# Reading order of the token operand in the 512-column matrix products of a two-block float32 model

## The chip, the cores and the metric

The kernel is one program on one core of a Trainium2 chip. The metric is the device time of one execution in microseconds (us); lower is better. TensorE (PE) multiplies matrices, VectorE (DVE) and ScalarE (ACT) do elementwise work, GpSimd (POOL) a few masks and powers, and SyncE (SP) starts the transfers from memory. SBUF is the on-chip memory that the engines read, PSUM the one that TensorE writes.

## What is computed

A token matrix of 256 tokens by 1024 features goes through a first block (gated pooling and forgetting attention) and a second block of two layers, with four feed-forward parts among other things. Nearly all of the work of the products that are changed lies in those four:

```python
D_MODEL, SEQ, D_FF = 1024, 256, 2816

def swiglu(x, w_gu, w_down):
    gate, up = jnp.split(x @ w_gu, 2, axis=-1)
    return (jax.nn.silu(gate) * up) @ w_down
...
x = x + 0.5 * swiglu(rms_norm(x, ffn1_norm[l]), ffn1_w_gu[l], ffn1_w_down[l])
```

All data are float32. The kernel multiplies in a faster TensorE format (`F32R`, "fp32r" in the rows) of lower precision, and gets precision back by splitting each operand in a high part (the value rounded to that format) and a low part (what is left): a product is then w_hi·x_hi + w_lo·x_hi + w_hi·x_lo.

## The kernel before

A weight matrix arrives in units of up to 11 blocks of 128 x 128. SP brings two units at a time into `raw`; ACT rounds a unit into `w_hi` (L594), DVE subtracts and leaves the rest in `w_lo` (L1157), four units deep each. TensorE then runs through the blocks `k` of a unit and adds their products up in one of four PSUM banks of 512 columns, `main0` to `main3`. A unit's end lets ACT and DVE take the result and prepare a later unit.

There are two ways to make the three products of a block:

- **Triples** (`triple`, L2138 to L2140): three products of 256 columns (the tokens), into the same 256 columns of a bank. They are used outside the feed-forward parts, and in a few units in them.
- **Pairs**: one product of `w_hi` with high and low tokens together, 512 columns, that puts w_hi·x_hi in columns 0 to 255 of the bank and w_hi·x_lo in 256 to 511; then one product of `w_lo` with the high tokens, 256 columns, added to columns 0 to 255. The two halves of the bank are added when ACT and DVE take them out. `project_halves` (L2165 and L2167) does this for gate and up, 8 blocks to a unit; `down` in `ffn` (L2523 and L2525) for the second matrix, 11 blocks to a unit.

The tokens lie in SBUF in two ways. For gate and up it is `xs`, of shape 128 x 8 x 2 x 256: for one block `k`, the 256 high tokens (1024 bytes of each partition) and right behind them the 256 low ones, so that the 512 columns are one run of addresses. For down it is `h_both`, of shape 128 x 2 x 22 x 256: the low tokens of a block lie 22528 bytes behind its high ones, so that the 512 columns are two runs. In both, the destination is one run of 512 columns. `enter` (the first two units of two of the feed-forward parts) makes pairs as well, with code of its own that the change doesn't touch.

The order of the instructions is written out by hand for each engine; semaphores tie the engines together. TensorE waits for `lo_ready` at the start of a unit and for `evac` where it takes a bank again.

Of the kernel before, what the change touches and what calls it, by code (L numbers as in the profile page):

```python
# [16 lines left out]
KC = D // P  # L17
# [5 lines left out]
FT = FF // P  # L23
# [134 lines left out]
def program(nc, dram, out):  # L158
    with ExitStack() as ctx:
# [7 lines left out]
        xs, _ = place("xs", at + 32, [P, KC, 2, SEQ], F32R)  # L167
# [6 lines left out]
        w_hi, at = place("w_hi", at, [P, RING, UNIT], F32R)  # L174
# [18 lines left out]
        h_both, at = place("h_both", free0, [P, 2, FT, SEQ], F32R)  # L193
# [227 lines left out]
        def piece(tensor, u, b, n=1):  # L421

            return tensor[:, u % RING, b * P:(b + n) * P]
# [1705 lines left out]
        def _(pe):  # L2129
# [6 lines left out]
            def triple(dst, a_hi, a_lo, b_hi, b_lo, first, last):  # L2136
# [2 lines left out]
                pe.matmul(dst, a_lo, b_hi, start=False, stop=False)  # L2139
                return pe.matmul(dst, a_hi, b_lo, start=False, stop=last)  # L2140

            def unit_begin(u, off=0):
                pe.wait_ge(lo_ready, u + 1 + off)

# [14 lines left out]
            def project_halves(u, bank, off=0, first=None):  # L2159

                unit_begin(u, off)
                for k in range(KC):
                    if first is not None:
                        pe.wait_ge(xg_ready, first + k + 1)
                    pe.matmul(bank[:, :], piece(w_hi, u, k), xs[:, k], start=k == 0, stop=k == KC - 1,  # L2165
                              skip_group_check=True)
                    ins = pe.matmul(bank[:, 0:SEQ], piece(w_lo, u, k), xs_hi[:, k], start=False, stop=k == KC - 1,  # L2167
                                    skip_group_check=True)
                unit_end(ins)
# [176 lines left out]
            bank = side[2]  # L2346
# [10 lines left out]
            for u in range(40):  # L2357
# [16 lines left out]
                if 8 <= u < 12:  # L2374
# [9 lines left out]
                    for kk in range(2):  # L2384
                        k = 2 * j + kk
# [104 lines left out]
            def ffn(which):  # L2490
                f, u0, t0 = FFNS.index(which), first_unit("w_gu_" + which), FIRST_TILE["gu_" + which]

                def turn(i, first=None):
                    if first is not None and which != "a1":
                        enter(u0, [bank_of(t0 + j) for j in range(2)], (xs_hi, xs_lo) if which == "b2" else (xs,), first,
                              2 if which == "b2" else 1, None if which == "b2" else FFN_NORM[which])
                    for j in range(2 if first is not None and which != "a1" else 0, 4):
                        if which == "b2" and first is not None:
                            project(u0 + j, bank_of(t0 + j)[:, 0:SEQ], xs_hi, xs_lo,
                                    within=(KC - 2, lambda: norm_sum(FFN_NORM[which])) if j == 2 else None)  # L2500
                        else:
                            project_halves(u0 + j, bank_of(t0 + j, i * 4), i * 4, first if j == 0 else None)
                        if first is not None and which == "a1" and j == 0:
                            norm_sum(FFN_NORM[which])

                if which != "b1":
                    turn(0, XG0["ffn_" + which])
                with pe.Fori(0 if which == "b1" else 1, (FT - FFN_FIRST[which]) // 2) as i:
                    turn(i)
                u0, t0 = first_unit("w_down_" + which), FIRST_TILE["down_" + which]  # L2510

                def down(m, i=0, joined_parts=True):
                    bank = bank_of(t0 + m, i * 4)
                    for j in range(2):
                        u = u0 + 2 * m + j
                        pe.wait_ge(h_ready, f * FT + FT // 2 + j * (FT // 2 - 2))
                        unit_begin(u, i * 8)
                        for b in range(FT // 2):
                            k = j * (FT // 2) + b
                            if k >= FT - 2:  # L2520
                                pe.wait_ge(h_ready, f * FT + k + 1)
                            if joined_parts:
                                pe.matmul(bank[:, :], piece(w_hi, u, b), h_both[:, :, k, :], start=k == 0,  # L2523
                                          stop=k == FT - 1, skip_group_check=True)
                                ins = pe.matmul(bank[:, 0:SEQ], piece(w_lo, u, b), h_hi[:, k, :], start=False,  # L2525
                                                stop=k == FT - 1, skip_group_check=True)
                            else:
                                ins = triple(bank[:, 0:SEQ], piece(w_hi, u, b), piece(w_lo, u, b),
                                             h_hi[:, k, :], h_lo[:, k, :], k == 0, k == FT - 1)
                        unit_end(ins)  # L2530

                if which == "b2":
                    for m in range(KC):
                        down(m, joined_parts=m < KC - 1)
                else:
                    with pe.Fori(0, 2) as i:
                        for m in range(4):
                            down(m, i)
# [583 lines left out]
```

## Time and profile before

| | |
|---|---|
| time, median of 3 runs | 1196.64 us (1196.5 to 1197.19) |
| span of the profiled execution, first to last instruction | 1195.0 us |
| the median less that span (start and end around it; the profiled execution's own total is not listed) | 1.6 us |
| TensorE busy with matmuls | 1187.3 us (99%), 7956 of them |
| DVE busy | 934.7 us (78%) |
| ACT busy | 730.4 us (61%) |
| mean granted TensorE clock | 0.999 of full speed |

A matmul's row gives its start and a modelled duration, from the first column that goes in to the last that comes out; the next one starts before it ends. How fast TensorE gets on is therefore read from one start to the next, not from the durations. Where a group's busy time is given for products that overlap the next of the same group, it is the time that the whole sequence took.

### The profile page before, as it was taken

How to read it: one execution, taken by the hardware profiler on the slowest of the kernel's cores; microseconds unless marked ns; L12 is line 12 of the kernel's file. 1: busy time of each engine (PE TensorE's matmuls, PEld its weight loads, DVE VectorE, ACT ScalarE, POOL GpSimd, SP SyncE). 2: the span in 40 equal slices, each digit the busy share in tenths (PEclk: the TensorE clock that was granted, in tenths of full speed). 3: DMA queues.
4: the chain of work that ended last, by engine and by line, in shares of the span. 5: the costliest groups of instructions: out<-in, count | busy, mean ns of one | idle time of the engine just before them, and what ended most of it. 6: DMA issues, size and time to landing. Idle time of an engine off the chain costs nothing.

```text
span 1195.0 us, 22393 instructions
## 1 busy us (share of the span) xinstructions
PE 1187.3 (99%) x7956; PEld 1089.4 (91%) x7956; DVE 934.7 (78%) x1617; ACT 730.4 (61%) x1211; POOL 77.9 (7%) x91
## 2 busy tenths in 40 slices
PE   9999999999999999999999999999999999999998
PEld 9899999888888999999888889988888989888887
DVE  7766788988876788688988767888876787888853
ACT  7564746666654588567666645666664567666642
POOL 4460000000000000610000000000000000000000
PEclk9999999999999999999999999999999999999999
DMA  8545655554654445115555743655663423555730
GB/s 329 184 142 187 232 189 177 186 208 176 230 214 154 141 170 188 41 36 177 211 178 204 258 151 123 211 176 194 219 239 135 150 91 125 195 205 178 255 131 36
DMA packets 48143, 209.92 MB, mean 176 GB/s; under 512 B 3486, under 2 KB 4908, under 8 KB 43596
## 3 DMA queue, kind: packets, MB, share of 16 engines
q1 hardware_dynamic: 46720, 204.96, 48.7%
q10 hardware_dynamic: 1356, 4.07, 1.0%
q8 instruction: 41, 0.67, 0.2%
q14 instruction: 26, 0.21, 0.0%
HBM read 207.90 MB, written 1.13 MB: 175 GB/s over the span
## 4 chain that ended last, share of the span: by engine, by line
PE 93%; DVE 4%; ACT 1%; issue 1%; DMA 1%; DVEq 0%; SPq 0%; ACTq 0%
PE main L2165 25%; PE main L2167 13%; PE main L2523 13%; PE main L2138 8%; PE main L2139 8%; PE main L2140 8%; PE main L2525 7%; DVE w_lo L1157 1%; PE side L2303 1%; PE main L2566 1%; PE side L2566 1%; PE side L2277 1%; PE main L2682 1%; PE main L2854 1%; PE main L2858 1%
## 5 line engine op out<-in xcount | busy, mean ns | idle before, releaser
L1157 DVE TENSOR_TENSOR w_lo<-raw,w_hi 128x1024 fp32r<-128x1024 f32 (+3 forms) x365 | 466.8, 1287 | 5.0 <-ACT w_hi L594 3.8
L2165 PE MATMUL main<-xs,w_hi 128*128 128x512 f32 x1328 | 461.3, 390 | 0.2 <-DVE xs L1191 0.2
L594 ACT ACTIVATE w_hi<-raw 128x1024 fp32r<-128x1024 f32 (+2 forms) x363 | 402.5, 1111 | 68.3 <-PE main L2140 53.0
L2167 PE MATMUL main<-xs,w_lo 128*128 128x256 f32 x1328 | 374.5, 282 | 0.0
L2165 PEld LDWEIGHTS main<-xs,w_hi 128*128 128x128 f32 x1328 | 249.2, 188 | 53.2 <-DVE w_lo L1157 0.7
L2167 PEld LDWEIGHTS main<-xs,w_lo 128*128 128x128 f32 x1328 | 251.0, 189 | 0.0
L2523 PE MATMUL main<-h_both,w_hi 128*128 128x512 f32 x682 | 236.6, 390 | 0.0
L2525 PE MATMUL main<-h_both,w_lo 128*128 128x256 f32 x682 | 192.3, 282 | 0.0
L2523 PEld LDWEIGHTS main<-h_both,w_hi 128*128 128x128 f32 x682 | 128.0, 188 | 26.8
L2525 PEld LDWEIGHTS main<-h_both,w_lo 128*128 128x128 f32 x682 | 128.9, 189 | 0.0
L2138 PE MATMUL main<-xs,w_hi 128*128 128x256 f32 x368 | 105.4, 286 | 0.0
L2139 PE MATMUL main<-xs,w_lo 128*128 128x256 f32 x368 | 102.9, 280 | 0.0
L2140 PE MATMUL main<-xs,w_hi 128*128 128x256 f32 x368 | 102.7, 279 | 0.0
L2138 PE MATMUL main<-xg,w_hi 128*128 128x256 f32 (+1 forms) x288 | 82.7, 287 | 0.3 <-DVE w_lo L1157 0.3
L2139 PE MATMUL main<-xg,w_lo 128*128 128x256 f32 (+1 forms) x288 | 81.0, 281 | 0.0
L2140 PE MATMUL main<-xg,w_hi 128*128 128x256 f32 (+1 forms) x288 | 81.0, 281 | 0.0
L1511 DVE TENSOR_TENSOR hid<-main,hid 128x256 f32<-128x256 f32 x84 | 35.6, 424 | 50.9 <-ACT hid L800 50.9
L800 ACT ACTIVATE hid<-main 128x256 f32<-128x256 f32 x84 | 32.3, 384 | 69.9 <-PE main L2167 69.9
L612 ACT ACTIVATE xs<-x,par 128x256 fp32r<-128x256 f32 (+1 forms) x48 | 23.9, 508 | 78.5 <-DVE x L1484 66.9
L2138 PEld LDWEIGHTS main<-xs,w_hi 128*128 128x128 f32 x368 | 69.2, 188 | 0.4 <-issue 0.2
L2139 PEld LDWEIGHTS main<-xs,w_lo 128*128 128x128 f32 x368 | 69.2, 188 | 0.1
L2140 PEld LDWEIGHTS main<-xs,w_hi 128*128 128x128 f32 x368 | 69.2, 188 | 0.0
(505 smaller groups left out, 1869.6 us busy)
## 6 DMA issues: line engine op xcount, KB each, us to landing
raw<-in_w_gu_a SPq DMA_DIRECT2D x44, 1024.0 KB, 5.2
raw<-in_w_gu_b SPq DMA_DIRECT2D x44, 1024.0 KB, 5.2
raw<-in_w_down_a SPq DMA_DIRECT2D x16, 1408.0 KB, 6.1
raw<-in_w_down_b SPq DMA_DIRECT2D x16, 1408.0 KB, 6.0
raw<-in_w_in SPq DMA_DIRECT2D x15, 1024.0 KB, 5.4
raw<-in_w_in_a SPq DMA_DIRECT2D x13, 1024.0 KB, 5.2
raw<-in_w_gates SPq DMA_DIRECT2D x4, 1024.0 KB, 5.1
raw<-in_w_up SPq DMA_DIRECT2D x4, 1024.0 KB, 5.2
```

Of the source, the lines that this page charges most:

```text
L594: act.activation(w_hi[:, u % RING, 0:n], raw[:, s % RAW, u % 2, 0:n], ACT.Copy).then_inc(hi_ready, 1)
L800: act.activation(dst, main[(t0 + n) % 4][:, SEQ:2 * SEQ], ACT.Copy).then_inc(low_half, 1)
L1157: return dve.tensor_tensor(dst, src, hi.bitcast(F32), ALU.subtract)
L1511: dve.tensor_tensor(dst, main[(t0 + n) % 4][:, 0:SEQ], dst, ALU.add).then_inc(evac, 1)
L2138: pe.matmul(dst, a_hi, b_hi, start=first, stop=False)
L2139: pe.matmul(dst, a_lo, b_hi, start=False, stop=False)
L2140: return pe.matmul(dst, a_hi, b_lo, start=False, stop=last)
L2165: pe.matmul(bank[:, :], piece(w_hi, u, k), xs[:, k], start=k == 0, stop=k == KC - 1, skip_group_check=True)
L2167: ins = pe.matmul(bank[:, 0:SEQ], piece(w_lo, u, k), xs_hi[:, k], start=False, stop=k == KC - 1, skip_group_check=True)
L2523: pe.matmul(bank[:, :], piece(w_hi, u, b), h_both[:, :, k, :], start=k == 0, stop=k == FT - 1, skip_group_check=True)
L2525: ins = pe.matmul(bank[:, 0:SEQ], piece(w_lo, u, b), h_hi[:, k, :], start=False, stop=k == FT - 1, skip_group_check=True)
L2566: ins = pe.matmul(dst[:, i * P:(i + 1) * P], lhs(i), rhs(i), start=first, stop=True, skip_group_check=not first)
```

## The change

Two helpers turn the operands' views. `parts_in_turn(v, n)` reads `n` high tokens, then the `n` low ones that belong to them, then the next `n` high ones, and so on; `in_turn(bank, n)` writes in the same order, so that each result lands in the column where it landed before. Gate and up use runs of 32 columns (16 runs to a product), down runs of 128 (4 runs). Number, kind and order of the instructions of all engines stay as they are, and so do the places of all data.

```diff
+            def in_turn(bank, n):
+                return bank[:, :].rearrange("p (i b n) -> p b i n", i=2, n=n)
+
+            def parts_in_turn(v, n):
+                return v.rearrange("p i (b n) -> p b i n", n=n)
...
-                    pe.matmul(bank[:, :], piece(w_hi, u, k), xs[:, k], start=k == 0, stop=k == KC - 1,
+                    pe.matmul(in_turn(bank, 32), piece(w_hi, u, k), parts_in_turn(xs[:, k], 32), start=k == 0, stop=k == KC - 1,
                               skip_group_check=True)
                     ins = pe.matmul(bank[:, 0:SEQ], piece(w_lo, u, k), xs_hi[:, k], start=False, stop=k == KC - 1,
                                     skip_group_check=True)
...
                             if joined_parts:
-                                pe.matmul(bank[:, :], piece(w_hi, u, b), h_both[:, :, k, :], start=k == 0,
-                                          stop=k == FT - 1, skip_group_check=True)
+                                pe.matmul(in_turn(bank, 128), piece(w_hi, u, b), parts_in_turn(h_both[:, :, k, :], 128),
+                                          start=k == 0, stop=k == FT - 1, skip_group_check=True)
```

## Rows read from the trace of the kernel before

**Rows 1.** Page, part 1: busy us (share of the span) xinstructions
```profile
PE 1187.3 (99%) x7956; PEld 1089.4 (91%) x7956; DVE 934.7 (78%) x1617; ACT 730.4 (61%) x1211; POOL 77.9 (7%) x91
```

**Rows 2.** Page, part 4: the chain that ended last
```profile
PE 93%; DVE 4%; ACT 1%; issue 1%; DMA 1%; DVEq 0%; SPq 0%; ACTq 0%
```

**Rows 3.** Page, part 5: the four products of pairs; busy, mean ns | idle before
```profile
L2165 PE MATMUL main<-xs,w_hi 128*128 128x512 f32 x1328 | 461.3, 390 | 0.2 <-DVE xs L1191 0.2
L2167 PE MATMUL main<-xs,w_lo 128*128 128x256 f32 x1328 | 374.5, 282 | 0.0
...
L2523 PE MATMUL main<-h_both,w_hi 128*128 128x512 f32 x682 | 236.6, 390 | 0.0
L2525 PE MATMUL main<-h_both,w_lo 128*128 128x256 f32 x682 | 192.3, 282 | 0.0
```

**Rows 4.** Busy time by stretch, gate and up: PE, PEld, DVE, ACT, POOL, PEclk, DMA, GB/s
```profile
230.00:330.00 100.00, 100.00 (x579) 88.67 (x578) 85.16 (x148) 64.03 (x110) 0.00 (x0) 1.00 0.59 209
```

**Rows 5.** Products on xs (L2165) that started in 230 to 330: ns min/median/max, first, last
```profile
L2165 PE MATMUL main<-xs,w_hi x290: 390/390/390, 229.8 to 329.9; 128*128 128x512 f32 x145
```

**Rows 6.** Timeline of PE, first and last of those 290: start us, us
```profile
229.75 0.39 PE L2165 MATMUL main<-xs,w_hi 128*128 128x512 f32 x1
...
329.94 0.39 PE L2165 MATMUL main<-xs,w_hi 128*128 128x512 f32 x1
```

**Rows 7.** Products on h_both (L2523) in 342 to 398, and their first and last
```profile
L2523 PE MATMUL main<-h_both,w_hi x160: 390/390/390, 341.7 to 396.8; 128*128 128x512 f32 x160
...
341.73 0.39 PE L2523 MATMUL main<-h_both,w_hi 128*128 128x512 f32 x1
...
396.85 0.39 PE L2523 MATMUL main<-h_both,w_hi 128*128 128x512 f32 x1
```

**Rows 8.** Timeline of PE, two pairs of gate and up
```profile
299.78 0.39 PE L2165 MATMUL main<-xs,w_hi 128*128 128x512 f32 x1
300.01 0.28 PE L2167 MATMUL main<-xs,w_lo 128*128 128x256 f32 x1
300.13 0.39 PE L2165 MATMUL main<-xs,w_hi 128*128 128x512 f32 x1
300.36 0.28 PE L2167 MATMUL main<-xs,w_lo 128*128 128x256 f32 x1
```

**Rows 9.** Timeline of PEld (weight loads) in the same stretch
```profile
300.13 0.19 PEld L2167 LDWEIGHTS main<-xs,w_lo 128*128 128x128 f32 x1
300.36 0.19 PEld L2165 LDWEIGHTS main<-xs,w_hi 128*128 128x128 f32 x1
```

**Rows 10.** Timeline of PE, triples on xg: first products of triple 1 and 30
```profile
99.91 0.28 PE L2138 MATMUL main<-xg,w_hi 128*128 128x256 f32 x1
...
110.06 0.28 PE L2138 MATMUL main<-xg,w_hi 128*128 128x256 f32 x1
```

**Rows 11.** The same on cat_hi_a, cat_lo_a: triple 1 and triple 56
```profile
530.15 0.29 PE L2138 MATMUL main<-cat_hi_a,w_hi 128*128 128x256 f32 x1
...
549.59 0.28 PE L2138 MATMUL main<-cat_hi_a,w_hi 128*128 128x256 f32 x1
```

**Rows 12.** The same with weights as columns, tokens held: triple 1 and triple 14
```profile
208.04 0.28 PE L2138 MATMUL main<-w_hi,mem_hi 128*128 128x256 f32 x1
...
212.66 0.28 PE L2138 MATMUL main<-w_hi,mem_hi 128*128 128x256 f32 x1
```

## The prediction

> **What bounds the kernel now.** I read the busy shares first: TensorE has a matmul under way for 1187.3 of 1195.0 us, DVE for 78%, ACT for 61% [rows 1]. That alone doesn't say that TensorE is the limit, so the chain that ended last comes next: 93% of it is TensorE, 4% DVE [rows 2]. In a stretch of gate and up, 230 to 330 us, TensorE is never idle, DVE is busy 85.16 of 100 us, ACT 64.03, and the granted clock is 1.00 of full speed, that is the 2.4 GHz level [rows 4]. The four lines of the pairs had 0.2 us of idle time before them in all [rows 3]. So the time is the sum of the steps from one product's start to the next, and what the change does to the time is what it does to that step.
>
> The steps are read from starts. The 290 products on `xs` between 229.75 and 329.94 us make 289 pairs in 100.19 us, 346.68 ns each [rows 5, 6]. The 160 products on `h_both` from 341.73 to 396.85 us make 159 pairs in 55.12 us, 346.67 ns each [rows 7]. The whole kernel agrees: the busy time of the 512-column products, which overlap from pair to pair, is 461.3 us for 1328 (347.4 ns each, waits included) and 236.6 us for 682 (346.9 ns) [rows 3]. Within a pair some 230 ns pass from the 512-column start to the 256-column one and some 120 ns from there to the next pair [rows 8]. The 768 columns of a pair need 768 / 2.4 = 320.0 ns at the granted clock. So 26.7 ns of each pair is over-time; over 1328 + 682 = 2010 pairs that is 53.7 us. The change can't take away more than this by reading the same columns in another order.
>
> **The change part by part.** It adds and removes no instruction, transfer or wait, and no data move to another place. It changes two things in 2010 products.
>
> *Reading.* Each product's columns are read in more runs. Call the passage from one run to the next a break. For `xs` there were none and there are 15; for `h_both` there was one (from the high tokens to the low ones, 22528 bytes on) and there are three. That is 15 x 1328 + 2 x 682 = 21,284 more breaks. What does a break cost? The trace has the comparison: a pair on `xs` without a break takes 346.68 ns, a pair on `h_both` with one takes 346.67 ns [rows 5 to 7]. The rounding of the starts to 0.01 us leaves 0.03 ns open in the first and 0.06 ns in the second, so a break costs at most 0.08 ns, and at most 0.08 x 21,284 = 1.7 us in all. I take zero, because the two sorts of pairs agree.
>
> *Writing.* The destination was one run of 512 columns everywhere and becomes 16 runs (gate and up) or 4 (down): 15 x 1328 + 3 x 682 = 21,966 breaks. No product of before writes with a break inside it, so this is bounded by neighbours. From below: nothing, as on the reading side; a gain is treated with the first rival. From above: a break can't well cost more than a whole new product with new weights does. A triple of 256-column products on `xg` takes (110.06 - 99.91) / 29 = 350.0 ns [rows 10], 116.7 ns a product of which 106.7 are columns: 10.0 ns of over-time per product start. At 10.0 ns a break it would be +220 us. Between 0 and 10 ns I take zero: it is the value of the nearest row, a break within one product, while the upper end is that of another event. A price in between, one column time a break, is the second rival.
>
> On the writing side stands also a rule of the Trainium skill, in "Advanced Engine Details and Errata", section "Memory Cachelines": PSUM is reached in lines of two float32 values, and "any non-contiguous AP significantly slows down matmuls". No row before has such a destination. The same section asks for every two consecutive elements to be contiguous, and runs of 32 and 128 columns meet that, so by this reading the sum stays at zero; by the first sentence taken literally it is the last rival below.
>
> *Other engines.* ACT and DVE read the bank after the pair's last product, and the results lie where they lay. If TensorE gets slower they wait more; if it gets faster by 2%, DVE's 85% in gate and up becomes 87%, so nothing else would take over at once [rows 4].
>
> Sum: 1195.0 + 0 (0 to 1.7 for reading) = 1195.0 us of span, and with the 1.6 us by which the runs' median stands above the span, 1196.6 us.
>
> **The rivals.**
>
> *Faster: part of the over-time goes away.* The 26.7 ns are not a fixed price. Products of the same shape at the same clock take 350.0 ns a triple on `xg` [rows 10], (549.59 - 530.15) / 55 = 353.5 ns on `cat_hi_a` and `cat_lo_a` [rows 11], and (212.66 - 208.04) / 13 = 355.4 ns where weights are the columns and tokens are held [rows 12]. Only what is read from where differs. A weight load runs beside each product from its start on [rows 8, 9], so both readings share something that depends on addresses, and an order that takes high and low tokens in turn goes through the addresses in another rhythm. The smallest step between these rows is about 3.4 ns for 768 columns. One such step down in each pair gives 2010 x 3.4 = 6.8 us, 1189.8 us; two give 1183.0 us; one in gate and up alone 4.5 us. Against it: the pairs take 346.7 ns on both token arrays, though one lies in one run and the other in two, and the step is the same in each of hundreds of pairs. The chance is 0.30, of which 0.06 for more than two steps.
>
> *Slower: a break costs one column time.* If the next run's first column goes in one clock late, because reading or writing has to set up a new start, a break costs 1 / 2.4 = 0.42 ns. On the writing side's count that is 21,966 x 0.42 = 9.2 us, 1205.8 us: 8.3 us of it in gate and up, where a product would take 6.3 ns more. It decides against no change from 2.4 / 21,966 = 0.11 ns a break. For it speaks that the trace shows no destination with breaks, and that 16 runs in 213 ns ask for a new start every 13 ns; against it that the one break in the reading of `h_both` costs nothing that can be seen. The chance is 0.19.
>
> *Slower: the other rhythm costs a step.* The first rival with the other sign: 3.4 ns more a pair, 1203.4 us. The rows give the sign no preference, except that the place with the largest over-time per column in them is the triple of rows 12, not the pair, so there is room upwards. The chance is 0.07.
>
> *Slower by far: a destination in runs is written at a much lower rate.* At the upper end of the writing side, 10.0 ns a break, it would be 1196.6 + 220 = 1416 us. The row of `h_both` can't exclude it, since its break is in the reading only. The chance is 0.02. This is the result that the skill's sentence quoted above would give if it held for runs of any length.
>
> *The change does nothing*, because the lists of addresses are worked off column by column and a run's end is no event at all. That is the forecast's own mechanism and gives its time.
>
> **How the numbers follow.** No change 0.42 (1196.6 us; by its own bounds 1194.3 to 1199.0), faster 0.30, slower by a column time 0.19, slower by a step 0.07, far slower 0.02. About 0.2%, 2.4 us, is what a measurement of this kernel can tell from no change. Faster by more than that is 0.30, within it 0.42, slower 0.28. The likeliest case gives 1196.6 us. The range reaches down to the two steps of the first rival, 1183, and up to the column time a break, 1206; beyond it lie 0.06 below and, with half of the spread around the column time, some 0.10 above.
>
> **What would show it.** In the profile of the changed kernel the starts of the 512-column products decide. If I am right, 290 products on `xs` still take 100.19 us and the busy time of that group stays at 461.3 us, that of `h_both` at 236.6 us. If a break costs a column time, a pair of gate and up takes 352.9 ns and one of down 347.9: gate and up suffer, down hardly. If over-time is given back, the pairs come below 346.7 ns, and the triples, which are not touched, stay at 350.0 and 353.5 ns. A difference between gate and up and down tells how the length of a run matters. The step from a 512-column start to the 256-column one must change and the other way round not, if the cost sits in the product with runs. What would make the forecast wrong is above all that a rhythm can't be read from rows of another rhythm, and that nothing before shows a destination in runs.

## The result: 8.6 us slower

| | before | after |
|---|---|---|
| time, median of 4 runs | 1196.59 us (1196.50 to 1197.19) | 1205.20 us (1205.07 to 1205.43) |
| ratio | 1 | 1.0071, interval 1.0059 to 1.0084 |
| span of the profiled execution | 1195.0 us | 1203.4 us |
| products of gate and up, 1328 of 512 columns: busy with their sequence | 461.3 us | 470.0 us |
| products of down, 682 of 512 columns: the same | 236.6 us | 236.6 us |

The change costs 0.7%, clear of what a measurement can tell from nothing, where no change was forecast. The forecast was wrong.

### The profile page after: what moved, and what is told of

It is laid out like the page before. It is cut to its first block, busy times and chain, and to the rows that moved or that the text cites. A ratio compares the mean times of both kernels' runs of the same rounds, so it can differ in the third digit from the quotient of the medians.

```text
span 1203.4 us, 22393 instructions
## 1 busy us (share of the span) xinstructions
PE 1196.4 (99%) x7956; PEld 1088.1 (90%) x7956; DVE 935.7 (78%) x1617; ACT 729.4 (61%) x1211; POOL 77.9 (6%) x91
## 4 chain that ended last, share of the span: by engine, by line
PE 95%; DVE 3%; ACT 1%; issue 1%; DVEq 0%; ACTq 0%
PE main L2171 26%; PE main L2173 13%; PE main L2529 13%; PE main L2138 8%; PE main L2140 8%; PE main L2139 8%; PE main L2531 7%; PE side L2309 1%; DVE w_lo L1157 1%; PE main L2572 1%; PE side L2572 1%; PE side L2283 1%; PE main L2688 1%; PE main L2860 1%; PE main L2864 1%; PE main L2862 1%
## 5 line engine op out<-in xcount | busy, mean ns | idle before, releaser
L2171 PE MATMUL main<-xs,w_hi 128*128 128x512 f32 x1328 | 470.0, 398 | 0.1
L2173 PE MATMUL main<-xs,w_lo 128*128 128x256 f32 x1328 | 371.9, 280 | 0.0
L2171 PEld LDWEIGHTS main<-xs,w_hi 128*128 128x128 f32 x1328 | 249.3, 188 | 63.3 <-DVE xs L1191 0.5
L2173 PEld LDWEIGHTS main<-xs,w_lo 128*128 128x128 f32 x1328 | 249.3, 188 | 0.0
L2529 PE MATMUL main<-h_both,w_hi 128*128 128x512 f32 x682 | 236.6, 390 | 0.0
L2531 PE MATMUL main<-h_both,w_lo 128*128 128x256 f32 x682 | 192.3, 282 | 0.0
L2529 PEld LDWEIGHTS main<-h_both,w_hi 128*128 128x128 f32 x682 | 128.0, 188 | 26.9
L2531 PEld LDWEIGHTS main<-h_both,w_lo 128*128 128x128 f32 x682 | 128.9, 189 | 0.0
```

The costliest lines, as they stand in the source:

```text
L2171: pe.matmul(in_turn(bank, 32), piece(w_hi, u, k), parts_in_turn(xs[:, k], 32), start=k == 0, stop=k == KC - 1, skip_group_check=True)
L2529: pe.matmul(in_turn(bank, 128), piece(w_hi, u, b), parts_in_turn(h_both[:, :, k, :], 128), start=k == 0, stop=k == FT - 1, skip_group_chec ...
```

## The profile after

The page's busy shares, the chain that ended last, and the groups of the pairs (L2171 and L2173 are the former L2165 and L2167, L2529 and L2531 the former L2523 and L2525; the columns are those of [rows 1 to 3]):

```profile
PE 1196.4 (99%) x7956; PEld 1088.1 (90%) x7956; DVE 935.7 (78%) x1617; ACT 729.4 (61%) x1211; POOL 77.9 (6%) x91
...
PE 95%; DVE 3%; ACT 1%; issue 1%; DVEq 0%; ACTq 0%
...
L2171 PE MATMUL main<-xs,w_hi 128*128 128x512 f32 x1328 | 470.0, 398 | 0.1
...
L2173 PE MATMUL main<-xs,w_lo 128*128 128x256 f32 x1328 | 371.9, 280 | 0.0
...
L2529 PE MATMUL main<-h_both,w_hi 128*128 128x512 f32 x682 | 236.6, 390 | 0.0
L2531 PE MATMUL main<-h_both,w_lo 128*128 128x256 f32 x682 | 192.3, 282 | 0.0
```

TensorE still sets the end, and all of the loss is in gate and up: 470.0 - 461.3 = 8.7 us against the first of [rows 3]. Down is where it was, to 0.1 us. The span grew by 8.4 us, a little less: TensorE was idle for 7.0 us (1203.4 - 1196.4) where it had been for 7.7.

The steps are read from starts, as in [rows 5, 6]. The timeline of PE in gate and up, with the number of 512-column products that started in 230 to 330 us (the two ends stand on the same product line, 283 pairs apart):

```profile
L2171 PE MATMUL main<-xs,w_hi x284: 397/397/398, 229.8 to 329.8; 128*128 128x512 f32 x142
...
229.76 0.40 PE L2171 MATMUL main<-xs,w_hi 128*128 128x512 f32 x1
230.00 0.28 PE L2173 MATMUL main<-xs,w_lo 128*128 128x256 f32 x1
230.12 0.40 PE L2171 MATMUL main<-xs,w_hi 128*128 128x512 f32 x1
...
329.76 0.40 PE L2171 MATMUL main<-xs,w_hi 128*128 128x512 f32 x1
```

100.00 us for 283 pairs are 353.4 ns a pair, where it was 346.7. The whole of it lies between the start of the 512-column product and that of the next one, some 236 ns where some 228 were; the other step got a nanosecond shorter. ACT and DVE only wait longer for it: ACT's wait for `hid` in all, 69.9 us before, is

```profile
ACT hid L800 <- PE main L2173: 76.8, 76, 1.1
```

**How the experiments are read.** The four feed-forward parts a1, a2, b1 and b2 run one after the other, and several kernels below do another thing in each. One view gives a row for each part: the busy time of the 512-column products alone, with their number. Since they overlap from pair to pair, this is the time of the whole sequence of pairs. The difference to the same row of the kernel before, divided by the number, is what a pair costs more. The columns of a row are: window, its length, PE busy with the number of products, PEld busy with the number of loads, clock, DMA share, GB/s. Gate and up, before and then after:

```profile
212.00:340.00 128.00, 122.62 (x352) 66.04 (x352) 1.00 0.57 202
555.00:680.00 125.00, 116.68 (x336) 63.08 (x336) 1.00 0.57 201
760.00:880.00 120.00, 110.98 (x320) 60.08 (x320) 1.00 0.59 206
1010.00:1130.00 120.00, 111.00 (x320) 60.04 (x320) 1.00 0.58 200
```

```profile
212.00:340.00 128.00, 124.88 (x352) 66.09 (x352) 1.00 0.56 198
555.00:684.00 129.00, 118.92 (x336) 63.08 (x336) 1.00 0.56 198
760.00:888.00 128.00, 113.11 (x320) 60.07 (x320) 1.00 0.57 201
1015.00:1140.00 125.00, 113.12 (x320) 60.08 (x320) 1.00 0.56 198
```

So the change costs 6.4, 6.7, 6.7 and 6.6 ns a pair in a1 to b2. (In a1 the first products wait for weights anyway, which hides a part.) The numbers of the other kernels are given as such differences. Down has rows of the same kind; before, in a1 and b2, and after, in a1:

```profile
334.00:400.00 66.00, 61.06 (x176) 33.02 (x176) 1.00 0.49 175
1124.00:1184.00 60.00, 53.43 (x154) 28.89 (x154) 1.00 0.30 111
```

```profile
336.00:402.00 66.00, 61.07 (x176) 33.04 (x176) 1.00 0.49 173
```

Each kernel up to the last two (down128 and turns64) ran once. Where a kernel below changes gate and up with a view or for reading or writing alone, down is as in the kernel before.

## Experiments

Two theories stood at the start. The second rival of the prediction: each break between runs costs a column time. It gives nearly the right total, 1205.8 us, but 1.25 ns a pair for down, which took none. And the third: another rhythm of addresses costs a step. Beside them stood the question which side it is, reading or writing.

### Reading or writing

```diff
-                    pe.matmul(in_turn(bank, 32), piece(w_hi, u, k), parts_in_turn(xs[:, k], 32), ...
+                    pe.matmul(bank[:, :], piece(w_hi, u, k), parts_in_turn(xs[:, k], 32), ...      # read32
...
+                    pe.matmul(in_turn(bank, 32), piece(w_hi, u, k), xs[:, k], ...                  # write32
```

> Gate and up read in turns of 32 columns but write one run of 512; down as in the kernel before. The low and high sums so land in other columns than the later steps take them from, so the values are not the reference's; the work is the same. Theory R (the cost sits in reading): a pair of gate and up takes 353.4 ns as in the changed kernel, time about 1205. Theory W (it sits in writing PSUM in runs): 346.7 ns as before, time about 1196.6. If each side has a part, in between.

> The other half alone: gate and up read one run of 512 columns and write in turns of 32 (values not the reference's, for the same reason). Theory R: 346.7 ns a pair, about 1196.6. Theory W: 353.4 ns a pair, about 1205.

Read32 took 1205.57 us, write32 1196.69 us, beside 1197.28 us for the kernel before on the same chip. The rows of b1 and b2 of read32:

```profile
760.00:888.00 128.00, 113.11 (x320) 60.06 (x320) 1.00 0.57 201
1015.00:1140.00 125.00, 113.13 (x320) 60.07 (x320) 1.00 0.57 197
```

and of write32:

```profile
760.00:880.00 120.00, 110.98 (x320) 60.04 (x320) 1.00 0.59 206
1010.00:1130.00 120.00, 111.00 (x320) 60.08 (x320) 1.00 0.57 201
```

The cost is in the reading, all of it. A destination in 16 runs of 32 columns costs nothing that can be seen. So one of the two things that by the prediction's last sentence could make it wrong, a destination in runs, was free. The other one was the rhythm of the reading.

### The length of a run

```diff
+GU_RUN = {'a1': 8, 'a2': 16, 'b1': 64, 'b2': 128}
+DOWN_RUN = {'a1': 8, 'a2': 16, 'b1': 32, 'b2': 64}
...
-                    pe.matmul(in_turn(bank, 32), piece(w_hi, u, k), parts_in_turn(xs[:, k], 32), ...
+                    pe.matmul(in_turn(bank, n), piece(w_hi, u, k), parts_in_turn(xs[:, k], n), ...
...
-                                pe.matmul(in_turn(bank, 128), piece(w_hi, u, b), parts_in_turn(h_both[:, :, k, :], 128),
+                                pe.matmul(in_turn(bank, DOWN_RUN[which]), piece(w_hi, u, b), parts_in_turn(h_both[:, :, k, :], DOWN_RUN[which]),
```

> Both sides in turns, with another run length in each of the four feed-forward parts: gate and up 8, 16, 64, 128 columns (a1, a2, b1, b2), down 8, 16, 32, 64. Read from starts part by part. A fixed price per break (6.7 ns over 15 breaks, 0.45 ns each) gives gate and up 375, 360.6, 349.8, 348.0 ns a pair and down about the same for its lengths. A price that only short runs have, since they are too short to hide a new start, gives 346.7 for 64 and 128 and more than 353 for 16 and 8. A step in the rhythm of stalls gives values in steps of about 3.4 ns, not in proportion to the breaks. If what matters is the array read (xs against h_both) and not the length, down stays at 346.7 at 32 as well.

The kernel short is the same with 4, 2, 32, 16 in gate and up and 4, 2, 8, 32 in down:

> Reading and writing in turns, all results right. Gate and up 4, 2, 32, 16 columns in a1, a2, b1, b2; down 4, 2, 8, 32. So far 32 took 353.4 ns a pair, 16 and 8 both about 358. Theory F counts lines of 64 bytes: 64 for runs of 16 (each in two lines) and 64 for runs of 8 (one each), 128 for 4, 256 for 2; from 48 lines = +6.7 ns and 64 = +11.5 on, 128 lines give +30 ns or more and 256 far more. Theory S (a price per short run) gives, from +6.7 for 16 runs and +11.5 for both 32 and 64 runs, no clear law. Theory M (only a rhythm) gives values that stay within some 12 ns of 346.7 whatever the number of runs, until runs get shorter than 16 bytes. The 16 and 32 columns on the other array repeat what was seen on the first.

The sweep took 1208.82 us, short 1268.55 us. A pair costs more by, in ns (differences as explained; those of down against its own rows of before, 61.06, 61.06, 61.06 and 53.43 us for 176, 176, 176 and 154 products):

| run, columns | 128 | 64 | 32 | 16 | 8 | 4 | 2 |
|---|---|---|---|---|---|---|---|
| run, bytes | 512 | 256 | 128 | 64 | 32 | 16 | 8 |
| gate and up (xs) | 0.0 | 0.0 | 6.7 | 10.8 | 11.2 | 21.7 | 100.5 |
| down (h_both) | 0.1 (changed kernel) | 0.0 | 6.6 | 11.1 | 11.7 | 22.2 | 101.0 |

The rows of gate and up in the sweep, runs of 8, 16, 64 and 128 columns:

```profile
212.00:342.00 130.00, 126.57 (x352) 66.96 (x352) 1.00 0.56 195
555.00:690.00 135.00, 120.31 (x336) 64.07 (x336) 1.00 0.56 200
760.00:892.00 132.00, 110.98 (x320) 60.08 (x320) 1.00 0.60 207
1020.00:1142.00 122.00, 111.01 (x320) 60.04 (x320) 1.00 0.57 198
```

The rows of down in the sweep, runs of 8, 16, 32 and 64 columns:

```profile
338.00:405.00 67.00, 63.12 (x176) 33.48 (x176) 1.00 0.47 165
680.00:752.00 72.00, 63.01 (x176) 33.56 (x176) 1.00 0.45 161
884.00:955.00 71.00, 62.23 (x176) 33.03 (x176) 1.00 0.46 161
1134.00:1196.00 62.00, 53.43 (x154) 28.89 (x154) 1.00 0.32 117
```

Three things follow. The array doesn't matter: both cost the same at the same length. That down was free in the changed kernel is due to its 128 columns alone. And a price per break falls: 7 and 15 breaks are 0 and 6.7 ns, 31 and 63 breaks both some 11 ns. Something happens between runs of 256 bytes and of 128. In both kernels the destination is cut into runs as short as those of the reading. For 32 columns write32 showed that this is free; below 32 columns the two sides were not separated.

### Length, or the order of addresses

Turns of 64 columns, 256 bytes, have a property that turns of 32 lack. The low tokens lie a multiple of 256 bytes behind the high ones in both arrays (1024 and 22528). With runs of 256 bytes each address therefore follows the last one modulo 256 bytes just as in one run; with runs of 128 the low run starts 128 bytes back. Of the powers of two only 256 fits both: from the first high run to the first low one, turns of 64 skip 768 bytes, 3 x 256, which breaks the order modulo 512 and is free, and turns of 32 skip 896 bytes, 7 x 128, which keeps the order modulo 128 and costs. Three theories were set against each other: lines of 64 bytes that runs touch (F), the order of addresses modulo 256 bytes (M), and short runs as such (S). The kernels rhythm and offsets change nothing but the view of the tokens, in elements of 4 bytes: a start and pairs of stride and count. In all kernels with such a `VIEW` the first pass through the units of a1 and a2 keeps the usual view, 32 of 352 and 16 of 336 pairs. So for a pair that is changed the differences given for a1 and a2 are to be taken times 1.10 and 1.05.

```diff
+VIEW = {"a1": (0, [[64, 8], [288, 2], [1, 32]]), "a2": (0, [[96, 8], [1, 64]]),        # rhythm
+        "b1": (8, [[32, 8], [256, 2], [1, 32]]), "b2": (8, [[1, 512]])}
...
+VIEW = {"a1": (16, [[32, 8], [256, 2], [1, 32]]), "a2": (4, [[1, 512]]),               # offsets
+        "b1": (4, [[64, 4], [256, 2], [1, 64]]), "b2": (0, [[64, 4], [256, 2], [1, 64]])}
...
-                    pe.matmul(in_turn(bank, 32), piece(w_hi, u, k), parts_in_turn(xs[:, k], 32), ...
+                    pe.matmul(bank[:, :], piece(w_hi, u, k), tokens(k, view), ...
```

> Only the reading of the 512-column product of gate and up is changed, another way in each feed-forward part (all but its first turn); destination one run, down as before; the tokens read are not the right ones, so the values aren't the reference's. a1: runs of 32 columns whose starts go on as in one run when taken modulo 256 bytes. a2: runs of 64 columns, each starting 128 bytes modulo 256 off where one run would be. b1: turns of 32 columns as in the changed kernel, all 32 bytes further on, so that each run fills two lines of 64 bytes exactly. b2: one run of 512, 32 bytes further on. Theory F (what costs is how many lines of 64 bytes the runs touch: 33 for one run, 48 for turns of 32 that start in mid-line): 353.4, 346.7 (40 lines), 346.7 (32 lines), 346.7 ns a pair. Theory M (what costs is a rhythm of addresses that differs from one run's modulo 256 bytes): 346.7, over 346.7, 353.4, 346.7. Theory S (a run shorter than some 64 columns costs, wherever it lies): 353.4, 346.7, 353.4, 346.7.

> As the kernel rhythm, with other starts (values not the reference's). a1: turns of 32 columns, 64 bytes further on. a2: one run of 512, 16 bytes further on. b1: turns of 64 columns, 16 bytes further on. b2: turns of 64 columns at the usual place. Theory F: 353.4 in a1 (the runs straddle lines as before), 346.7 in the others (at most 40 lines). Theory M: 353.4 in a1, 346.7 in the others. Theory S: the same as M. The four tell above all whether the start alone, by 16 and 64 bytes, moves a pair that one kind of run leaves at 346.7.

They took 1201.46 and 1200.24 us beside 1196.63. The rows of rhythm, a1 to b2:

```profile
212.00:340.00 128.00, 122.62 (x352) 66.09 (x352) 1.00 0.58 201
555.00:680.00 125.00, 118.81 (x336) 63.95 (x336) 1.00 0.55 195
760.00:886.00 126.00, 113.11 (x320) 60.58 (x320) 1.00 0.58 203
1010.00:1136.00 126.00, 111.49 (x320) 60.23 (x320) 1.00 0.56 195
```

The first row decides. In a1 a product is read in 16 runs of 32 columns, with as many breaks as in the changed kernel, but each run starts where the last one ended modulo 256 bytes: 122.62 us, to the hundredth what one run takes. In a2 the runs are twice as long, with 7 breaks, but each starts 128 bytes off: 6.3 ns a pair more (6.7 for each of the 320 changed ones). Theory M said so of both; S had them the other way round, and F failed in all three of a1, a2 and b1 (in b1 runs that fill lines of 64 bytes exactly still cost 6.7 ns). In b2 one run that starts 32 bytes further on cost 1.5 ns, which no theory had. Offsets cost 8.4 (9.2 a changed pair), 0.1, 0.0 and 0.0 ns: turns of 64 are free at two starts, turns of 32 are not at any of three. That the start moves the price from 6.7 to 9.2 ns theory M doesn't explain.

### What one jump costs

```diff
+VIEW = {"a1": (0, [[288, 2], [1, 256]]), "a2": (0, [[160, 4], [1, 128]]),
+        "b1": (0, [[48, 16], [1, 32]]), "b2": (0, [[80, 8], [1, 64]])}
```

> Only the reading of the 512-column product of gate and up (all turns but the first), destination one run, values not the reference's. Each run starts further on than where the last ended. a1: two runs of 256, the second 128 bytes further (1 jump, and one back to the usual place at the next product). a2: four runs of 128 columns, each 128 bytes further (3 jumps and 1 back). b1: 16 runs of 32, each 64 bytes further (15 jumps). b2: 8 runs of 64, each 64 bytes further (7 jumps). Theory J (each jump of 128 bytes modulo 256 costs 6.67 / 8 = 0.83 ns, since turns of 32 have 8 of them and turns of 64 none): 348.3, 350.0, then for jumps of 64 bytes at the same price 359.2 and 352.5, at half of it 352.9 and 349.6. Theory Q (pairs come in steps of 6.67 ns, 346.7, 353.3 or 360.0, whatever the number of jumps): 353.3 in a1 and a2, and 353.3 or 360.0 in b1 and b2.

It took 1202.83 us beside 1196.90. The rows, a1 to b2:

```profile
212.00:340.00 128.00, 124.33 (x352) 66.02 (x352) 1.00 0.58 198
555.00:682.00 127.00, 118.80 (x336) 63.11 (x336) 1.00 0.57 196
765.00:886.00 121.00, 112.04 (x320) 60.12 (x320) 1.00 0.60 207
1012.00:1136.00 124.00, 112.42 (x320) 60.06 (x320) 1.00 0.56 194
```

These are 4.9, 6.3, 3.3 and 4.4 ns a pair more; for a changed pair 5.3 and 6.6 in a1 and a2. Both theories fall: one jump in the middle of a product, with the one back at its end, already costs 5.3 ns, 15 jumps of 64 bytes cost 3.3. The price is not a sum of prices of jumps. What holds over all kernels with runs of 32 columns or more is only this: at the usual place and start, each pattern that breaks the order modulo 256 bytes cost 3.3 to 6.7 ns, and none that keeps it cost anything.

### The place of the tokens

```diff
-        xs, _ = place("xs", at + 32, [P, KC, 2, SEQ], F32R)
+        xs, _ = place("xs", at, [P, KC, 2, SEQ], F32R)
```

Place0 is the changed kernel with this line, plain_place0 the kernel before with it.

> The changed kernel with xs 32 bytes lower, so that the token runs start on the same residue of 64 bytes as the weights (xs was 32 bytes off it). If the price comes from short runs that start in the middle of a line of 64 bytes or more, a pair of gate and up falls from 353.4 to 346.7 ns and the time to about 1196.6. If a break costs the same wherever it falls, 353.4 ns and about 1205. The triples on xs may move too; that then tells how much the place alone matters.

> The kernel before with xs 32 bytes lower. It is the base that the changed kernel at this place lacks, where pairs took 353.4 in a2 and b2 and 360.0 ns in a1 and b1. If the place alone costs (weights and tokens then start on the same residue of 64 bytes), its pairs take 353.4 ns or more with one run, and the turns there cost nothing or one step. If they take 346.7, turns of 32 cost one or two steps at this place too, and lines that are filled exactly don't help: theory F falls.

They took 1211.63 and 1203.55 us. The rows of plain_place0, a1 to b2:

```profile
212.00:340.00 128.00, 122.62 (x352) 66.00 (x352) 1.00 0.58 202
555.00:682.00 127.00, 118.75 (x336) 63.13 (x336) 1.00 0.56 195
765.00:886.00 121.00, 110.99 (x320) 59.84 (x320) 1.00 0.60 209
1014.00:1136.00 122.00, 113.11 (x320) 60.13 (x320) 1.00 0.57 196
```

Against the kernel before, a pair costs, in ns:

| | a1 | a2 | b1 | b2 |
|---|---|---|---|---|
| plain_place0, one run | 0.0 | 6.2 | 0.0 | 6.6 |
| place0, turns of 32 | 12.6 | 6.6 | 13.3 | 6.6 |
| so the turns at this place | 12.6 | 0.5 | 13.2 | 0.0 |

32 bytes decide over 6.9 us of the kernel with one run (1203.55 - 1196.63). The pairs of a2 and b2 are 4.2 us of it. The rest lies outside the pairs: the 368 triples that read `xs` took 2.6 us more by their starts (132.2 us before, 134.8 with the lower place), 12 of them in a row 358.4 ns each where they took 350.1. The place of the kernel before is the better one, and the turns don't help at the other place; lines that are filled exactly don't either. Why the pairs of two parts suffer from the place and those of two don't is open. The third row shows that what the rhythm costs and what the place costs don't add up: where the place costs 6 ns already, turns of 32 cost 0.5 and 0.0 ns on top, and where it costs nothing, they cost 13. So the order modulo 256 bytes alone doesn't give the price.

A further run tried one run of 512 at four more starts, for the 512-column product alone:

```diff
+VIEW = {"a1": (16, [[1, 512]]), "a2": (24, [[1, 512]]), "b1": (32, [[1, 512]]), "b2": (48, [[1, 512]])}
```

> One run of 512 columns for the first product of gate and up, started 64, 96, 128 and 192 bytes further on (a1, a2, b1, b2); the rest as before (values not the reference's). So far 16 bytes gave 346.8 ns a pair and 32 bytes 348.3. Theory C expects that some of these starts give other values than 346.7, up or down, and that one below 346.7 would point to a faster place. Theory T: 346.7 to 348.3 in all.

It took 1198.92 us; 0.0, 0.1, 6.7 and 0.0 ns a pair more. The third has no break at all. It starts 128 bytes off the 256-column products between which it stands, so the order is broken from product to product; that this is the cause is a reading and was not tested by itself. That 64, 96 and 192 bytes cost nothing there shows once more that the price is no sum over jumps. None is below one run at the usual start, so no place was found that beats the kernel before.

### Do the weight loads take part?

The prediction's first rival rested on this: a weight load runs beside each product [rows 8, 9], and both readings get in each other's way.

```diff
+VIEW = {"a1": (None, (0, [[2, 128]]), (0, [[2, 128]])),                                # weights
+        "a2": (None, (32, [[1, 128]]), (32, [[1, 128]])),
+        "b1": ((0, [[32, 8], [256, 2], [1, 32]]), (32, [[1, 128]]), (32, [[1, 128]])),
+        "b2": ((32, [[32, 8], [256, 2], [1, 32]]), None, None)}
...
-                    pe.matmul(bank[:, :], piece(w_hi, u, k), tokens(k, view), ...
+                    pe.matmul(bank[:, :], held(w_hi, u, k, hi_view), tokens(k, view), ...
-                    ins = pe.matmul(bank[:, 0:SEQ], piece(w_lo, u, k), xs_hi[:, k], ...
+                    ins = pe.matmul(bank[:, 0:SEQ], held(w_lo, u, k, lo_view), xs_hi[:, k], ...
```

> Does the rhythm matter against the weight loads that run beside the products, or for the tokens alone? Only gate and up (all turns but the first), destination one run; values not the reference's, since other columns of tokens or weights are read. a1: tokens in one run, both weight loads take every second column (a stride of 8 bytes). a2: tokens in one run, both weight loads start 128 bytes further on. b1: tokens in turns of 32, both weight loads start 128 bytes further on. b2: tokens in turns of 32 that start 128 bytes further on, weights as usual. Theory C (token reads and weight reads get in each other's way, by their places modulo 256 bytes): a1 leaves 346.7 ns, since the weight reads have another rhythm; b1 and b2 are alike, the relative place being the same, and may differ from 353.4. Theory T (a rhythm of tokens costs by itself): a1 and a2 stay at 346.7 and b1 and b2 at 353.4.

It took 1203.97 us; 6.1 (6.7 a changed pair), 0.0, 6.7 and 6.7 ns. Mixed: a1 spoke for theory C (token and weight reads hinder each other), a2 and the sizes in b1 and b2 for theory T (the tokens' rhythm costs by itself). So the loads were made shorter (narrow) and given strides one by one (strides).

```diff
+VIEW = {"a1": (None, (0, [[1, 32]]), (0, [[1, 32]])),                                  # narrow
+        "a2": ((0, [[32, 8], [256, 2], [1, 32]]), (0, [[1, 32]]), (0, [[1, 32]])),
+        "b1": (None, (0, [[1, 64]]), (0, [[1, 64]])),
+        "b2": ((0, [[32, 8], [256, 2], [1, 32]]), (0, [[1, 64]]), (0, [[1, 64]]))}
...
+VIEW = {"a1": (None, (0, [[2, 32]]), (0, [[2, 32]])), "a2": (None, (0, [[3, 128]]), (0, [[3, 128]])),   # strides
+        "b1": (None, (0, [[2, 128]]), None), "b2": (None, None, (0, [[2, 128]]))}
```

> Shorter weight loads beside the same token reads. In gate and up (all turns but the first) each product holds only part of its 128 weight columns, and so fills only that many partitions of the bank (part of the result is left out): 32 weight columns in a1 and a2, 64 in b1 and b2; tokens in one run in a1 and b1, read in turns of 32 in a2 and b2, destination one run. The token columns stay 512 and 256. Theory C (token and weight reads get in each other's way): the over-time of a pair, 26.7 ns with 128 weight columns, shrinks with them, to about 7 to 10 ns with 32 and 13 to 16 with 64, and so does what the turns cost, 6.7 ns, to about 0 to 2 and 0 to 4. Theory T (a rhythm of tokens costs by itself): the turns still cost 6.7 ns, so a2 is 6.7 above a1 and b2 above b1, whatever the over-time does.

> Do weight reads take part? Tokens in one run everywhere, gate and up only (all turns but the first), values not the reference's. a1: 32 weight columns, every second one (both products; part of the result is left out). a2: 128 weight columns, every third (12 bytes apart). b1: only the w_hi loads take every second column. b2: only the w_lo loads do. Before: every second column of 128 in both gave 352.8 ns. Theory C (weight and token reads share something by address): the price differs with the stride and is less for b1 and b2 than for both, since each load runs beside one of the two products. Theory L (a load with a stride takes longer of itself and the next product starts later): with 32 columns it fits in easily, so a1 is 346.7, and b1 and b2 share the 6.1 ns.

Narrow took 1200.78 us. The first row is its weight loads of 32 columns in a1 (ns min/median/max), the others are the rows a1 to b2:

```profile
L2191 PEld LDWEIGHTS main<-xs,w_hi x300: 107/108/112, 226.2 to 329.8; 128*32 128x32 f32 x150
...
212.00:340.00 128.00, 122.54 (x352) 40.63 (x352) 1.00 0.58 202
555.00:680.00 125.00, 118.72 (x336) 38.16 (x336) 1.00 0.56 196
760.00:886.00 126.00, 111.00 (x320) 42.88 (x320) 1.00 0.59 207
1010.00:1136.00 126.00, 113.11 (x320) 42.88 (x320) 1.00 0.57 198
```

The loads take 108 ns where they took 188 [rows 9], and the busy time of PEld falls from 66.04 to 40.63 us in a1. Yet the pairs take what they took: -0.2 and +0.1 ns with tokens in one run, +6.1 and +6.6 ns with turns of 32. At the usual place neither the over-time of a pair nor the price of the rhythm depends on how long the weight loads read. Theory C, by which both shrink with the loads, falls; at the lower place of `xs` this was not tried. Nor did it matter where the weights lie against the tokens: both loads 128 bytes further on cost 0.0 ns (a2 of weights).

What a stride in the weights does is another thing. Strides took 1220.03 us, with -0.2, 63.0 (66 a changed pair), 4.4 and 0.0 ns a pair. In b1 only the w_hi loads have a stride, in b2 only the w_lo loads. First a load's row in a2, where every third column is taken, then one in b1:

```profile
L2191 PEld LDWEIGHTS main<-xs,w_hi x243: 253/255/255, 569.9 to 669.9; 128*128 128x128 f32 x122
...
L2191 PEld LDWEIGHTS main<-xs,w_hi x199: 193/195/198, 800.1 to 869.7; 128*128 128x128 f32 x199
```

A load with a stride takes longer of itself: the w_hi load 195 ns with 8 bytes and 255 with 12, where it takes 188 without; the w_lo load 198 with 8 bytes. By theory L the w_hi load, which starts with the short product of 256 columns, has only 118 ns until the next product starts and delays what follows, while the w_lo load has the long one, 228 ns, to hide in. B1 and b2 agree: 4.4 ns for the w_hi loads with a stride, 0.0 for the w_lo loads; and 32 columns with a stride (108 ns, a1) cost nothing. So a1 of the kernel weights needs no quarrel with the tokens. What L does not account for is the size: b1 and b2 were to share what both loads cost together, 6.7 ns for a changed pair, and have 4.4. In a2 both loads have a stride and the w_lo load, at 262 ns, no longer fits in 228 either, so the two shares aren't separated there. The timeline of a2, first products and then a load, has the delay behind the start of the long product, 0.30 us to the next start for the 0.23 of [rows 8], and beside it a w_lo load that starts 0.05 us after the product and not with it [rows 9]:

```profile
650.21 0.46 PE L2191 MATMUL main<-xs,w_hi 128*128 128x512 f32 x1
650.51 0.28 PE L2193 MATMUL main<-xs,w_lo 128*128 128x256 f32 x1
...
650.26 0.26 PEld L2193 LDWEIGHTS main<-xs,w_lo 128*128 128x128 f32 x1
```

### Down alone, and turns of 64, ten runs each

```diff
-                    pe.matmul(in_turn(bank, 32), piece(w_hi, u, k), parts_in_turn(xs[:, k], 32), ...
+                    pe.matmul(bank[:, :], piece(w_hi, u, k), xs[:, k], ...                         # down128
...
+                    pe.matmul(in_turn(bank, 64), piece(w_hi, u, k), parts_in_turn(xs[:, k], 64), ...   # turns64
```

> The part of the change in down alone: turns of 128 columns there, gate and up in one run. By the trace of the changed kernel its pairs take 346.73 ns against 346.67, so the time should be within 0.2% of the kernel before: 1196.6 to 1196.9 us by every theory that stands; only if the two parts act on each other (down's products leave the gate and up that follow in another rhythm) could it be more.

> The changed kernel with turns of 64 columns in place of 32 in gate and up; down in turns of 128 as there; all results right. One part of the sweep took 346.7 ns a pair with 64. If only the order of addresses modulo 256 bytes matters, the time is that of the kernel before, 1196.6 to 1196.9 us. If the number of breaks matters at all (7 in place of 15), half of the 8.6 us would be left, about 1200.9 us.

| | median of 10 runs | before on the same chip, 13 runs | ratio, interval |
|---|---|---|---|
| down128 | 1197.02 us | 1196.81 us | 1.0000 (0.9990 to 1.0009) |
| turns64 | 1196.94 us | 1196.90 us | 1.0002 (0.9992 to 1.0012) |

Both are the kernel before. Turns64 differs from the changed kernel in one number, 64 for 32, and has the 8.6 us back. High and low in turns cost nothing, turns of 128 bytes do. Its row of b1:

```profile
760.00:880.00 120.00, 110.98 (x320) 60.08 (x320) 1.00 0.59 207
```

## Why the prediction was wrong

- **TensorE is the bound, and the step from start to start is the time: right.** 1328 pairs at 6.4 to 6.7 ns more give the 8.7 us by which the group grew, and the span followed with 8.4.
- **Writing in runs costs nothing: right,** though taken against a range of 0 to 10 ns a break. Write32 shows it with 15 breaks a product. The Trainium skill's sentence that any non-contiguous pattern slows matmuls significantly (in "Advanced Engine Details and Errata", section "Memory Cachelines") doesn't hold for these destinations: 110.98 us for 320 pairs both ways. With that the last rival, far slower, falls too.
- **Reading breaks cost zero, at most 1.7 us: wrong, and this is the step that failed.** It took one kind of break as a measure for all. The one break in `h_both` [rows 5 to 7] leads 22528 bytes on, 88 times 256, and lands where the reading would have gone anyway modulo 256 bytes. It was the kind of break that is free. With runs of 128 bytes every second break, 8 of the 15, goes on 128 bytes off modulo 256, and the trace of before held no such break. The term that was put at zero measured 6.7 ns a product, 8.7 us in all. A comparison between two rows bounds only what differs between them, and between these rows the order modulo 256 bytes did not differ. The prediction's last sentence says itself that a rhythm can't be read from rows of another rhythm; its sum did so all the same.
- **Down, with two more breaks a product, costs nothing: right,** and for a reason the prediction didn't know.
- **The second rival, a column time a break,** had the time (1205.8 us) and not the cause: down would have paid 1.25 ns a pair and paid 0.0 to 0.1, and 15 breaks are free in the destination (write32) and, where they keep the order, in the reading (a1 of rhythm). That the measured time lies within the stated range is owed to this rival, whose mechanism is wrong, and is luck.
- **The third rival, another rhythm of addresses costs a step,** came nearest: a rhythm does cost. Its size was half of what was measured, 3.4 ns a pair against 6.7, and it charged down too, which paid nothing; that is why its 1203.4 us come so close. The 3.4 ns were said to be the smallest step between the rows; between 353.5 and 355.4 ns [rows 11, 12] it is 1.9. The rival got 0.07 where the same rhythm with the other sign got 0.30, though the prediction found no preference of sign in the rows. What it held against any such effect, that the step was the same on two arrays and in hundreds of pairs, spoke only of orders alike modulo 256 bytes.
- **The first rival, that a new rhythm gives over-time back, through the weight loads beside:** nothing of the kind. No pattern of tokens came out below 346.7 ns a pair, and the loads' length plays no part.

Open is what the 26.7 ns of over-time in each pair are, why places and orders cost in amounts near 6.7 ns (6.7, 13.3) in some kernels and in between in others, and what in the reading works by 256 bytes. That the order modulo 256 bytes decides between free and not free is shown at the usual place of `xs`, for runs of 32 columns and more; for shorter ones the length alone could do as much, and that wasn't separated.

## To carry to other kernels

Where a matmul of 512 float32 (fp32r) columns at the 2.4 GHz level reads its moving operand in several runs, make each run start where the last one ended modulo 256 bytes: runs of 256 bytes and distances that are multiples of 256 do it, and cost nothing here. The place of the array matters as much and follows no rule that was found: 32 bytes lower cost 6.2 to 6.6 ns a pair in two parts with one run, so compare both places by measurement. Runs in the destination, of 32 columns and more, were free. Before a row is used to bound the price of a new access pattern, write down the addresses of both and see in what they differ.

## What was not expected of the hardware

- Two runs, 128 bytes off the order, in one product of 512 columns cost 5.3 ns, 16 runs of 32 in order nothing.
- Moving the token array by 32 bytes cost 6.9 us: 4.2 us in the pairs of two of four parts that run the same code, 2.6 us in triples.
- A weight load of 32 columns in place of 128 took 108 ns for 188 and did not shorten a pair by more than 0.2 ns.
- A w_hi load with a stride of 8 bytes took 195 ns, with 12 bytes 255 ns; 12 bytes in both loads made a pair 66 ns longer.
